# Four modulation rows moved between the transposes of x at the head of a fused hybrid layer

## The reference, cut to what matters

```
mod = (silu(c) @ w_mod + b_mod);  sh_m, sc_m, gt_m, sh_f, sc_f, gt_f = split(mod, 6)
h = rms_norm(x, g_pre_mix) * (1 + sc_m) + sh_m
y = hybrid_mixer(h, w_in, ...)              # h @ w_in is 1024 x 7168, then convolutions,
                                            # a recurrence, gates and three projections
x = x + gt_m * rms_norm(y, g_post_mix)
h = rms_norm(x, g_pre_mlp) * (1 + sc_f) + sh_f
x = x + gt_f * rms_norm(relu(h @ w_mlp_up)**2 @ w_mlp_down, g_post_mlp)
```

## Time and profile before

| what | us |
|---|---|
| runs shown, median of 3 | 805.45 |
| runs shown, lowest and highest | 804.17 and 805.91 |
| the profiled execution: its own time | 805.0 |
| span of its trace | 803.4 |
| TensorE busy in that span | 793.8 |
| first product of the first units begins on TensorE | 21.42 |

### The profile page before, as it was taken

The page is one execution under the profiler, slowest core; times in us unless marked ns, Lnnn a source line. Parts: engine busy times, 40 slices in busy tenths (PEclk is TensorE's granted clock), DMA queues, the critical chain, the costliest instruction groups (busy, mean ns, idle before and its releaser), DMA issues.

```text
span 803.4 us, 12177 instructions
## 1 busy us (share of the span) xinstructions
PE 793.8 (99%) x4196; PEld 686.3 (85%) x4196; DVE 566.2 (70%) x714; ACT 475.8 (59%) x682; POOL 81.5 (10%) x94
## 2 busy tenths in 40 slices
PE   8999999999999999999999999999999999999996
PEld 8888788888888888888888889999999988888885
DVE  4776666666676556555587479877777598887778
ACT  6457777766664434444233566666666665555654
POOL 1540000001111011111111111101110000000000
PEclk8999999999999999999999999999999999999999
DMA  9961433327589999999977866778775495665502
GB/s 321 347 178 36 111 112 111 111 85 207 141 222 320 265 244 290 261 277 265 274 195 234 211 136 153 164 203 195 176 196 139 142 364 186 199 197 181 199 1 104
DMA packets 150949, 155.73 MB, mean 194 GB/s; under 512 B 5868, under 2 KB 118660, under 8 KB 150660
## 3 DMA queue, kind: packets, MB, share of 16 engines
q1 hardware_dynamic: 139300, 121.71, 49.2%
q0 software_dynamic: 11552, 33.57, 19.6%
q10 hardware_dynamic: 64, 0.02, 0.0%
HBM read 153.18 MB, written 35.65 MB: 235 GB/s over the span
## 4 chain that ended last, share of the span: by engine, by line
PE 97%; DVE 1%; DMA 0%; issue 0%; ACT 0%; ACTq 0%; DVEq 0%
PE ps L446 31%; PE ps L448 31%; PE ps L447 31%; PE ps L1684 1%; DVE xs L1631 1%; PE ps L1705 0%; DMA erows<-in_b_mod_dram 0%; DVE y L1621 0%; PE ps L1849 0%; PE ps L1692 0%; PE ps L1718 0%; DVE w_lo L1570 0%; PE ps L1822 0%; PE ps L1821 0%; PE ps L1731 0%
## 5 line engine op out<-in xcount | busy, mean ns | idle before, releaser
L446 PE MATMUL ps<-ht_hi,w_hi 128*128 128x512 f32 x448 | 175.5, 392 | 0.0
L447 PE MATMUL ps<-ht_lo,w_hi 128*128 128x512 f32 x448 | 174.7, 390 | 0.0
L448 PE MATMUL ps<-ht_hi,w_lo 128*128 128x512 f32 x448 | 174.5, 390 | 0.0
L1197 DVE TENSOR_TENSOR w_lo<-raw,w_hi 128x1024 fp32r<-128x1024 f32 x68 | 82.9, 1223 | 53.0 <-ACT w_hi L756 52.2
L446 PEld LDWEIGHTS ps<-ht_hi,w_hi 128*128 128x128 f32 x448 | 84.4, 188 | 18.6 <-issue 1.0
L448 PEld LDWEIGHTS ps<-ht_hi,w_lo 128*128 128x128 f32 x448 | 84.2, 188 | 17.8
L447 PEld LDWEIGHTS ps<-ht_lo,w_hi 128*128 128x128 f32 x448 | 84.2, 188 | 17.4
L756 ACT ACTIVATE w_hi<-raw 128x1024 fp32r<-128x1024 f32 x68 | 71.1, 1051 | 36.3 <-PE ps L448 24.5
L446 PE MATMUL ps<-w_hi,hd_hi 128*128 128x512 f32 x224 | 87.3, 390 | 0.0
L448 PE MATMUL ps<-w_hi,hd_lo 128*128 128x512 f32 x224 | 87.2, 389 | 0.0
L447 PE MATMUL ps<-w_lo,hd_hi 128*128 128x512 f32 x224 | 87.2, 389 | 0.0
(11 more groups left out here) (255 smaller groups left out, 1716.3 us busy)
## 6 DMA issues: line engine op xcount, KB each, us to landing
raw<-in_w_in_dram SPq DMA_DIRECT2D x48, 512.0 KB, 5.4
w_dn_sums<-in_w_mlp_down_dram POOLq DMA_DIRECT2D x48, 512.0 KB, 6.4
modraw<-in_w_mod_dram SPq DMA_DIRECT2D x32, 512.0 KB, 5.7
up_raw<-in_w_mlp_up_dram SPq DMA_DIRECT2D x56, 256.0 KB, 5.0
raw_y<-w_dn_sums SPq DMA_DIRECT2D x24, 512.0 KB, 4.2
mod_raw<-in_w_mod_dram SPq DMA_DIRECT2D x32, 256.0 KB, 7.3
w_dn_sums<-w_dn_sums POOLq DMA_DIRECT2D x16, 512.0 KB, 4.9
raw<-in_w_mlp_down_dram SPq DMA_DIRECT2D x12, 512.0 KB, 4.8
```

The lines of the kernel that those rows point to most:

```text
L446: nc.tensor.matmul(dst, l_hi, r_hi, start=first, stop=False, skip_group_check=chained)
L447: nc.tensor.matmul(dst, l_hi, r_lo, start=False, stop=False, skip_group_check=chained)
L448: return nc.tensor.matmul(dst, l_lo, r_hi, start=False, stop=last, skip_group_check=chained)
L1197: V.tensor_tensor(w_lo[:, slot, :], raw[:, slot, :], f(w_hi[:, slot, :]), ALU.subtract).then_inc(w_lo_ready, 1)
```

## The change

TensorE's order between the second block of x and `mod0_columns(0)` is written anew. Before: block 1, five unread transposes, block 2, pieces 0 and 1, block 3, pieces 2 and 3. After: block 1, piece 0, block 2, piece 1, two unread, piece 2, two unread, piece 3, block 3. The semaphores that each step waits for and gives are the same; no other engine's list changes.

```diff
-            for t in range(TB):
+            def x_transposes(t):
                 pe.wait_ge(x_norm, t + 1)
                 for k in range(X_BANKS):
                     last = nc.tensor.transpose(ps[:, k, t * P:(t + 1) * P], xs[:, t, k * P:(k + 1) * P], ident[:, :])
                     if t == TB - 1:
                         last.then_inc(x_tr, 1)
-                if t < 2:
-                    unread(5, last_tokens)
-                if t == 2:
-                    mod0_direct(range(0, 2))
-            mod0_direct(range(2, PE_ROWS))
+
+            x_transposes(0)
+            unread(5, last_tokens)
+            x_transposes(1)
+            mod0_direct(range(0, 1))
+            x_transposes(2)
+            mod0_direct(range(1, 2))
+            unread(2, last_tokens)
+            mod0_direct(range(2, 3))
+            unread(2, last_tokens)
+            mod0_direct(range(3, PE_ROWS))
+            x_transposes(TB - 1)
             pe.wait_ge(const_ready, 3)
             mod0_columns(0)
```

## The result

| | median of the runs | lowest and highest | runs |
|---|---|---|---|
| before | 805.27 us | 804.17, 806.28 | 22 |
| changed | 805.73 us | 804.59, 808.83 | 22 |

The ratio is 1.0012, 95% interval 1.0006 to 1.0017: a small loss, but one beyond the noise. The means of the runs differ by 0.87 us (806.07 against 805.21), the medians by 0.46. The forecast of 805.35 us was no change with a gain of 0.1 us. The time lies inside the range and within 0.2%, but on the other side.

The account below looks back on a forecast made before the run. TensorE, with 97% of the chain, was taken as the bound, meeting VectorE and full DMAs at the columns of group 1. Runs' median 805.45 less 0.1 us gain gave 805.35 us, range 803.8 to 807.3.

Parts of the forecast that it names:

- The clock held: From 16 to 18 us TensorE stays at full clock; the gain is lost waiting for VectorE, 0.1 us taken; chance 0.50.
- The bound: At the columns of group 1 TensorE and VectorE arrive together, 27.05 against 26.90; at most 0.15 us to gain.
- Removed and added transposes: Five unread transposes out, 0.54 us, four in, 0.44 us: TensorE's list 0.1 us shorter, no new waits.
- Block 3 last: x_tr comes 1.55 us later; ScalarE's idle 1.44 us takes most, modulation from 18.05, first large product near 20.2.
- My bound for the case: If the 1.55 us reach VectorE in full, its group 1 sum ends at 27.25: loss at most 0.35 us; chance 0.03.
- The clock falls all the same ... again no change: Columns, late and unread transposes keep their old costs from 15.7 to 21.6; TensorE arrives at 26.9; 805.4 us; chance 0.20.
- The hole: Clock falls while TensorE waits, 25.15 to 26.9, before the columns of group 1; 1.7 to 3.4 us slower; chance 0.17.

Follow-up runs that it names:

- spread_early: The kernel before, with two unread transposes behind piece 0 and two behind piece 1, between blocks 2 and 3: 805.83 us, ratio 1.0004.
- block3_early: The changed kernel with block 3 back ahead of pieces 2 and 3 and the unread transposes sent to another bank (output wrong): 804.76 us, ratio 0.9993.
- two_swap: The kernel before, with VectorE adding two pieces of group 1 first and SyncE loading its last two pieces ahead of block 2's weights: 805.55 us, ratio 0.9998.
- before_again: The kernel before, run again without an edit: 805.34 us, ratio 0.9999.
- after_look1: One single profiled execution of the changed kernel, without an edit: 806.56 us.
- order_only: The kernel before, with block 3 behind all four unbroken pieces and the unread transposes left where they were: 805.69 us, ratio 1.0007.
- keep_five: The changed kernel with the five unread transposes behind block 1 put back: 806.10 us, ratio 1.0010.
- swap_unread0: The kernel before with two_swap's edits and none of the twelve unread transposes ahead of the first large product: 806.03 us, ratio 1.0012.
- two_first: The changed kernel with VectorE adding two pieces of group 1, not one, ahead of the low part of block 0: 805.73 us, ratio 1.0008.
- fill_hole2: The changed kernel with ten unread transposes put in front of the columns of group 1: 807.80 us, ratio 1.0025.
- no_five_old_order: The kernel before without the five unread transposes behind block 1, block 3 in its old place: 805.42 us, ratio 1.0002.
- block3_middle: The changed kernel with block 3 ahead of pieces 2 and 3 and all four unread transposes right ahead of it: 805.41 us, ratio 0.9999.
- swap_unread4: The kernel before with two_swap's edits and four, not twelve, unread transposes ahead of the first large product: 805.27 us, ratio 1.0003.

## Why the prediction was wrong

**The clock held.** My likeliest case, with 0.50, had the stretch from 16 to 18 us at full clock and no low stretch. None of the 20 profiles shows that: each has at least 3.4 us at half in the head. The short stretch did not become more frequent with the change either: 10 of 33 runs are at 0.996 or more, against 62 of 129 before. Spreading on the old order did not raise the share (spread_early, 3 of 11); block3_early has 8 of 11, too few to tell.

**The bound.** Right that TensorE meets VectorE at the columns of group 1 and that the wait there swallows an earlier start; two_swap, in its class of the short low stretch, was 0.56 us faster once the pieces came earlier. What failed was to take the 0.15 us of one execution for the kernel's: before_again has TensorE 0.93 us late there, and the classes of before differ by 0.54 us. A second bound is missing from the sum. I let the columns of group 0 begin at 15.7 without asking when VectorE has its part of them. In the earlier trace rows's execution that was at 15.15 (14.39 + 0.76), but in nine of the 20 profiles TensorE waited for it, until 16.4 to 16.9, with block 3 last and with block 3 in its old place. Where this wait stands, block 3 may come last at no cost.

**Removed and added transposes.** The rows were right in size: 0.79 us for a piece, 0.28 for two unread ones with their gaps (I had 0.84 and 0.22). That the first pieces have landed by then held too.

**Block 3 last: the step that failed.** "Of the 1.55 us only 0.1 us is left." The mechanism was as I had it, and so was the order of waits. The size was not: I worked from an execution whose clock rose at about 9.2 (estimated from the 1.11 us of block 0, between 1.28 at half and 0.66 at full), where block 3 would end at 15.7. In the changed kernel's profiles it rose between about 9.2 and 12.0, estimated in the same way. Block 3 ended at 16.5 in the first and at 17.6 in after_look1, and the modulation began at 18.83 and 19.91 in their chains, not at 18.05. That took VectorE's 1.02 us of slack and in after_look1 1.3 us more (27.43 + 0.76 = 28.19 against 26.90). My bound for the case, 0.35 us (0.2 when counted from TensorE's 27.05 and not from VectorE's 26.90), let the whole 1.55 us through but nothing beyond it, and took the low part of block 0 at 0.69 us where it took 1.08. In the class of the shorter low stretch the loss is shown for order_only and keep_five, 0.8 and 1.2 us. For the changed kernel it is 0.37 us (805.47 against 805.10), or 0.2 without the run of 807.04, and neither is clear of the scatter of ten runs. In the class of the longer stretch order_only loses nothing (805.62 against 805.64).

**"The clock falls all the same ... again no change": the rival that failed.** I let the old fall, with the old costs behind it, follow the new list from 15.7. But block 3 and piece 3 can then stand behind the fall and cost double, and everything that hangs on `x_tr` waits for them. This is how I explain the group of 9 in 33 runs at 807.9 us, which makes most of the difference of the means. Leaving aside swap_unread0, where TensorE stands idle ahead of its first large product, low means are seen only with both parts of the change: block 3 last, and no unread transposes behind block 1. With both, 19 runs of 57 (changed, two_first, fill_hole2) have a mean clock of 0.993 or less; with block 3 last and the five kept 0 of 22 (order_only, keep_five); with the five gone and block 3 ahead of pieces 2 and 3 0 of 33 (no_five_old_order, block3_early, block3_middle). That is shown by counts; the early fall behind it was seen in one profile, that of fill_hole2.

**The hole.** The slower rival had the right price, 1.7 to 3.4 us, and nearly the right chance, for the wrong place. Filling the wait did not remove the group.

**What stays open.** No profile of the changed kernel itself caught an execution above 807 us. That the clock falls at 14.9, in piece 2, is shown for fill_hole2, whose list is the same up to there; for the changed kernel it is inferred from the mean clock and the time, and a usual fall with a late rise, as in swap_unread0, is a rival that no profile rules out. Nor is it explained why fill_hole2, which differs only behind 27 us, has 8 runs of 12 at 0.993 or less and the changed kernel 9 of 33. Why in some executions the clock rises and falls late and in others early is not settled. Easing the hand-over by rounding the first weights before ScalarE's copies was not tried: these weights lie over x, which TensorE must have read first. Nor was any version found that beats both kernels beyond the noise.

## What to carry to other kernels

Before moving a producer behind other work on the busiest engine, follow the whole chain that hangs on it in more than one execution; slack read from one profile, at one place of the clock's steps, may be gone in the next. Before ordering TensorE's work so as to hold a clock, ask what waits for the operand that is put back: here ScalarE and VectorE wait for block 3, and GpSimd behind them. And look at the list of all runs: a median that moves by 0.1% can hide one run in four that takes 2 us more.

## What the runs showed of the hardware

The clock's steps moved between executions of the same kernel: in the seven profiles of the changed one it rose between about 9.2 and 12.0 us (by the durations) and fell between 15.9 and 18.7 (by the granted clock), staying low for 3.4 or 6.8 us. Before the first rise TensorE had run nothing but transposes, and its transposes went from 0.21 to 0.11 us. In front of the first large product, where TensorE had nothing but unread transposes, taking them out (swap_unread0) left the clock low for 10.2 us in the one profile, until 26.8, and put 6 of 11 runs at a mean of 0.993 or less; with twelve (two_swap) and with four (swap_unread4) no run of 11 was. The Trainium skill ("TensorE: Matmul & The Clock Gate", Part 4, PE-mode transpose) states that full clock does not engage for transposes, as they are not counted as busy in the same way. These runs disagree with it.

The low part of block 0 (VectorE, L1273) took 0.69 us in twelve profiles and 1.08 or 1.09 in eight, and the two kinds part cleanly: in the eight GpSimd was still at work on the low part of the first weights (L704) when VectorE began, in the twelve it had ended. In after_look1:

```profile
20.00 1.82 POOL L704 TENSOR_TENSOR w_lo<-raw,w_hi 128x768 fp32r<-128x768 f32 x1 [18.33 <-ACT w_hi L780]
21.28 1.09 DVE L1273 TENSOR_TENSOR ht_lo<-xnt,ht_hi 128x512 fp32r<-128x512 f32 x1 [1.74 <-ACT ht_hi L788]
```

VectorE starts at 21.28, GpSimd ends at 21.82. Before the change ScalarE waited for the columns between rounding the weights, which releases GpSimd, and the modulation, which leads to VectorE's low part, and that kept the two apart (16.59 + 1.81 = 18.40, and 19.42). Where `x_tr` comes so late that this wait is gone, they meet, and VectorE's instruction takes 0.4 us longer. The Trainium skill ("SBUF — State Buffer", Who interferes with whom) states that a VectorE instruction with two inputs in SBUF contends with a GpSimd one that reads SBUF. The trace agrees: 1.09 us against 0.69. Of VectorE's two-port modes the same section of the Trainium skill says that whoever issues first holds the shared ports for the whole instruction. If that held here too, VectorE would end 0.69 us after 21.82, at 22.51; it ended at 22.37, though the ends of GpSimd's instructions are rough.
